# Weights' low parts on VectorE instead of GpSimd in the first seven heads of a delta-rule stage (Trainium2, one core)

## The reference, cut to what matters

```python
def gdn_mixer(h, w_in, w_conv, a_log, dt_bias, w_onorm, w_out):
    proj = h @ w_in                       # 512 x 1024 by 1024 x (4*1024 + 16)
    qkv, z, beta_logit, a_logit = jnp.split(proj, [3 * GDN_WIDTH, 4 * GDN_WIDTH, 4 * GDN_WIDTH + H], axis=-1)
    qkv = jax.nn.silu(causal_conv(qkv, w_conv))
    ...                                   # q and k are normalized per head
    o = chunk_gated_delta(q, k, v, g, beta)
    o = o * lax.rsqrt(jnp.mean(o * o, axis=-1, keepdims=True) + EPS) * w_onorm.astype(jnp.float32)
    return (o * jax.nn.silu(z)) @ w_out
```

## Time and profile before

| | |
|---|---|
| median of 3 runs | 2708.37 us (2707.45 to 2708.78) |
| the profiled execution | 2708.44 us, its span 2706.6 us |
| TensorE busy | 2662.2 us, 98% of the span |
| VectorE busy | 1387.7 us, 51% |
| ScalarE busy | 1226.5 us, 45% |
| GpSimd busy | 1075.8 us, 40% |
| granted TensorE clock | 0.999 of full speed |
| the longest chain | 70% TensorE, 6% VectorE, 2% ScalarE |

### The profile page before, as it was taken

The page is one execution under the profiler, slowest core; times in us unless marked ns, Lnnn a source line. Parts: engine busy times, 40 slices in busy tenths (PEclk is TensorE's granted clock), DMA queues, the critical chain, the costliest instruction groups (busy, mean ns, idle before and its releaser), DMA issues.

```text
span 2706.6 us, 42000 instructions
## 1 busy us (share of the span) xinstructions
PE 2662.2 (98%) x13886; PEld 2132.4 (79%) x13886; DVE 1387.7 (51%) x2452; ACT 1226.5 (45%) x1908; POOL 1075.8 (40%) x803
## 2 busy tenths in 40 slices
PE   8999999999999999999999999999999999999999
PEld 6887777777777777788887888887788877888886
DVE  7435333687778667787655221128753444222126
ACT  5334434455554555465544333235564553333234
POOL 5554333334333342443434544444412213544442
PEclk9999999999999999999999999999999999999999
DMA  4332222212021221222222333332211112333331
GB/s 159 102 101 82 82 70 77 71 55 63 31 62 51 65 74 60 86 78 70 72 68 86 101 101 93 93 112 86 78 39 49 61 31 70 109 94 93 99 102 55
DMA packets 59643, 211.89 MB, mean 78 GB/s; under 512 B 6688, under 2 KB 7072, under 8 KB 59552
## 3 DMA queue, kind: packets, MB, share of 16 engines
q1 hardware_dynamic: 57744, 206.89, 25.4%
q10 hardware_dynamic: 1520, 2.75, 0.3%
q0 software_dynamic: 288, 1.05, 0.1%
HBM read 208.57 MB, written 2.10 MB: 78 GB/s over the span
## 4 chain that ended last, share of the span: by engine, by line
PE 70%; DVE 6%; ACT 2%; issue 1%; DVEq 0%; ACTq 0%
PE bank L1329 18%; PE bank L1331 17%; PE bank L1330 17%; PE bank L3349 2%; PE bank L1458 2%; PE bank L3343 1%; PE bank L424 1%; PE bank L426 1%; PE bank L425 1%; DVE activations_low L454 1%; PE bank L1483 1%; PE bank L2199 1%; PE bank L3334 1%; PE bank L3337 1%; PE bank L3335 1%
## 5 line engine op out<-in xcount | busy, mean ns | idle before, releaser
L374 POOL TENSOR_TENSOR weights_low<-weights_raw,weights_high 128x512 fp32r<-128x512 f32 x776 | 1043.5, 1368 | 1439.7 <-ACT weights_high L358 1415.6
L1329 PE MATMUL bank<-activations_high,weights_high 128*128 128x512 f32 x2912 | 1176.3, 404 | 26.5 <-POOL weights_low L374 14.4
L1331 PE MATMUL bank<-activations_high,weights_low 128*128 128x512 f32 x2912 | 1138.6, 391 | 0.0
L1330 PE MATMUL bank<-activations_low,weights_high 128*128 128x512 f32 x2912 | 1137.4, 391 | 0.0
L1329 PEld LDWEIGHTS bank<-activations_high,weights_high 128*128 128x128 f32 x2912 | 548.4, 188 | 159.6 <-issue 18.9
L1331 PEld LDWEIGHTS bank<-activations_high,weights_low 128*128 128x128 f32 x2912 | 547.6, 188 | 116.3
L1330 PEld LDWEIGHTS bank<-activations_low,weights_high 128*128 128x128 f32 x2912 | 548.9, 189 | 108.1 <-issue 6.5
L358 ACT ACTIVATE weights_high<-weights_raw 128x1024 fp32r<-128x1024 f32 x384 | 403.8, 1053 | 283.6 <-PE bank L1331 276.7
L2980 DVE TENSOR_TENSOR mixed<-bank,mixed 128x512 f32 (+1 forms) x48 | 33.2, 692 | 193.9 <-PE bank L1331 193.9
L2924 ACT ACTIVATE to_split<-work 128x512 f32<-128x512 f32 x64 | 40.5, 632 | 181.5 <-DVE work L2966 181.5
L2966 DVE SCALAR_TENSOR_TENSOR work<-bank,rstd 128x512 f32<-128x512 f32 x64 | 44.2, 690 | 140.2 <-PE bank L1331 134.1
(11 more groups left out here) (471 smaller groups left out, 3300.3 us busy)
## 6 DMA issues: line engine op xcount, KB each, us to landing
weights_raw<-weights SPq DMA_DIRECT2D x388, 512.0 KB, 3.6
out_t<-residual SPq DMA_DIRECT2D x8, 256.0 KB, 2.1
residual<-x_t ACTq DMA_DIRECT2D x2, 512.0 KB, 7.8
residual<-x_t POOLq DMA_DIRECT2D x2, 512.0 KB, 10.0
work<-p_t ACTq DMA_DIRECT2D x2, 512.0 KB, 4.5
const<-consts SPq DMA_DIRECT2D x1, 713.0 KB, 12.8
const<-consts SPq DMA_DIRECT2D x1, 321.0 KB, 11.9
root<-positions ACTq DMA_DIRECT2D x1, 256.0 KB, 3.1
```

The source lines that it names most:

```text
L374: K.nc.gpsimd.tensor_tensor(K.w_lo[:, s, part], K.raw[:, s, part], K.w_hi[:, s, part].bitcast(F32), ALU.subtract).then_inc(K.job_sems["low ...
L1329: K.nc.tensor.matmul(dst, wh, K.act_hi[:, t, :], start=k == 0, stop=False)
L1330: K.nc.tensor.matmul(dst, wh, K.act_lo[:, t, :], start=False, stop=False)
L1331: ins = K.nc.tensor.matmul(dst, wl, K.act_hi[:, t, :], start=False, stop=k == len(tiles) - 1)
```

## The change

In the first seven heads (`more` is true) GpSimd no longer makes the low parts of the jobs r = 0 to 3. VectorE makes them, in the function `low_half(r, n, i)`: the same subtraction on the same half, with a wait on the high part and on the count of low halves so far. Two halves of r = 0 stand in levels 2 and 3, both of r = 1 behind the read of `ds6`, both of r = 2 behind the third state, both of r = 3 behind the normalization of the next query and key. GpSimd keeps the output's two products and its low part, and makes two low parts in head 7 as before. Nothing else changes; TensorE's and ScalarE's programs are the same.

```diff
--- before.py
+++ after.py
@@ -1773,9 +1773,11 @@
         weight_low(e, c0 + AHEAD + r)
 
     def head(i, more):
-        for r in range(4 if more else 2):
-            weight_low(e, c0 + 3 + AHEAD + r, i)
         if not more:
+            c = c0 + 3 + AHEAD
+            e.eng.wait_ge(K.job_sems["low"], i * (2 * SLOTS) + 2 * (c + SLOTS))
+            for r in range(2):
+                weight_low(e, c + r, i)
             return
         e.eng.wait_ge(K.sem("gdn_o_rstd"), i + 1)
         tt(b.o, b.o, b.r, ALU.mult).then_inc(K.sem("gdn_scaled"), 1)
@@ -1919,6 +1921,15 @@
     e.eng.sem_inc(K.sem("gdn_begin"), 1)
     e.eng.sem_inc(K.sem("gdn_head"), 1)
     normalize()
+
+    def low_half(r, n, i):
+
+        c = c0 + 3 + AHEAD + r
+        s, part = c % SLOTS, (slice(0, D // 2), slice(D // 2, D))[n]
+        e.eng.wait_ge(K.job_sems["high"], i * SLOTS + c + 1)
+        e.eng.wait_ge(K.job_sems["low"], i * (2 * SLOTS) + 2 * (c + SLOTS) + n)
+        v.tensor_tensor(K.w_lo[:, s, part], K.raw[:, s, part], K.w_hi[:, s, part].bitcast(F32), ALU.subtract) \
+            .then_inc(K.job_sems["low"], 1)
 
     def square_low(part, i):
 
@@ -1981,6 +1992,8 @@
             if l == 2:
                 ring.wait("qk", i)
                 ring.read("qk", v.tensor_tensor(b.qkt, by_block(ring.bank("qk")[:, :]), b.dt, ALU.mult))
+            if more and l in (2, 3):
+                low_half(0, l - 2, i)
             if l == 3 or more and l == 2:
                 take(conv, 1)
         ring.wait("vt", i)
@@ -2001,6 +2014,9 @@
         ring.wait("ds6", i)
         ring.read("ds6", v.tensor_scalar(b.sf[TOP, :, BOTTOM], by_chunk(ring.bank("ds6")[TOP, 0:NG * CH]), -1.0, None, ALU.mult))
         take(conv, 1)
+        if more:
+            low_half(1, 0, i)
+            low_half(1, 1, i)
         for c in range(NG):
             if c:
                 e.eng.wait_ge(K.sem("gdn_v_ready"), i * 3 + c)
@@ -2034,9 +2050,14 @@
                 if c == NG - 2:
                     e.eng.wait_ge(K.sem("gdn_state"), i * 3 + NG - 1)
                     e.eng.sem_inc(ring.free[ring.find("kst")[1]], 1)
+                    if more:
+                        low_half(2, 0, i)
+                        low_half(2, 1, i)
         if more:
             select(i + 1)
             normalize(i)
+            low_half(3, 0, i)
+            low_half(3, 1, i)
 
     head(0, True, True)
     with e.eng.Fori(0, H8 - 2) as k:
```

## The result

| | before | after |
|---|---|---|
| median, us | 2707.86 (22 runs, 2707.30 to 2708.86) | 2711.38 (22 runs, 2710.16 to 2714.03) |
| ratio to before, 95% interval | | 1.0014 [1.0009, 1.002] |
| profiled execution, us | 2708.44 | 2712.23 |
| its span, us; mean granted clock of TensorE | 2706.6; 0.999 | 2710.4; 0.998 |

A forecast was written before the change was run, and what follows sets the result against it. TensorE was taken to bound the loop, its parts covering the small chain almost without a gap. Terms 0 + 1.72 + 1.76 + 1.31 = 4.8 us on 2708.44 gave 2713.2 us, +0.18%, range 2711.0 to 2717.0.

The forecast's parts named there:

- GpSimd's relief is worth nothing: 72 us of halves leave GpSimd, idle for two thirds of the loop; nobody waited for them, so this counts nothing.
- A half takes 0.68, a pair 1.39: On VectorE, a half costs 0.68 us as L1926; a pair is 0.68 + 0.03 + 0.68 = 1.39 us.
- Heads 1 to 6 cost 0: In the loop VectorE's waits cover the halves, with 0.46, 0.27 and 0.73 us to spare at r = 1, 2, 3.
- the overrun rival: Loop halves run slower or register instructions between them take time: 2714.8, 2720 or 2729 us by size; chance 0.18.
- Nothing is early either: In heads 1 to 6 TensorE releases VectorE at each place, so the loop gains nothing: 0 per head.
- Head 0, 1.72 + 1.76 + 1.31: TensorE late by 1.72 us at part 17, 1.76 at part 25, and 1.31 for pair r = 3 before the next gram.
- the wide range: Whole-program time of 2711.0 to 2717.0 us, leaving out rivals faster and hidden and the far part of the overrun.
- its own case: The forecast of 2713.2 us itself, range 2712.2 to 2714.4, each of three terms within 0.3 us; chance 0.70.

The follow-up runs named there:

- before_hold: Kernel before, with GpSimd's low part of c0+5 held back ahead of head 0 until VectorE's first normalization is done: 2707.06 us, 0.9996.
- before_shift16: Kernel before, with 16 waits on a long-reached semaphore put into VectorE's head 0 where it is idle: 2707.41 us, ratio 1.0.
- again_r2: Kernel after, with one more unused 128x512 VectorE subtraction between the halves of r = 2 in heads 1 to 6: 2712.76 us, 1.0017.
- before_shift8: Kernel before, with 8 waits on a long-reached semaphore put into VectorE's head 0 where it is idle: 2706.49 us, 0.9997.
- only_head0: Kernel after, with only head 0's low halves on VectorE and those of heads 1 to 6 back on GpSimd: 2712.97 us, 1.0019.
- r1_earlier: Kernel after, with head 0's first half of r = 1 moved to level 3 from behind ds6: 2710.55 us, 1.0007.

## Why the prediction was right, and where it was off

- **GpSimd's relief is worth nothing:** right for the profiled execution of before, on which the forecast was built. VectorE's stretched lines did shrink (L1847 0.47 instead of 1.27), but each ran into a wait for TensorE. The Trainium skill, "GPSIMD Engine Reference", section "Specifications", says that the two engines share their memory interfaces. The traces agree with the stretching: L1966 takes 1.37 us beside GpSimd's low parts and 0.43 without. The relief isn't worth nothing in every execution: the stretch reached TensorE ahead of head 0, which the change doesn't touch, and once in the loop, 0.8 us, in two executions of kernels that leave these low parts to GpSimd (before_hold, before_shift16).
- **A half takes 0.68, a pair 1.39:** 0.65 to 0.70 for each of the 56; the pair 1.42 in the loop, 1.48 and 1.49 in head 0. The wait inside a pair costs a little more than taken. By the Trainium skill, "VectorE: DVE Perf Modes", section "The DRAIN you can't avoid", it would cost nothing. The traces disagree: from one half's start to the next's it is 0.60 us in again_r2, where what the second waits for is long there, and 0.73 inside a pair of the loop.
- **Heads 1 to 6 cost 0:** right, but tighter than worked out. The margins came out as 0.23 at r = 1 (0.46 forecast), 0 at r = 2 (0.27), 0.71 at r = 3 (0.73). The sum left out the gaps of 0.21 and 0.32 us ahead of a pair, though the overrun rival names such gaps. That rival's price, 0.6 us for each 0.1, was too high: of an overrun of 0.43 us at r = 2 TensorE paid 0.22 (again_r2). Its step for halves 0.4 us slower also leaves out that r = 3 would be 0.07 us late, 0.4 us more.
- **"Nothing is early either" in the loop:** by what the change moves, right; but 0.9 us came with the place of the loop's code (before_shift8).
- **Head 0, 1.72 + 1.76 + 1.31:** 1.6, 1.7 and 1.4, each at the part, the engine and the wait that was named. Sum 4.7 for 4.8.
- **What was missing in the sum** are effects of about 1 us that partly cancel: the clock's fall behind a stop, 1.6 us in the profiled execution of after, but not in every execution; the loop's code, -0.9; and the rest of the program behind the stage, -0.6 in after and -0.1 to -0.6 in the profiles of the other kernels with halves on VectorE, which no run took apart. 4.7 - 0.9 - 0.1 to 0.6 leaves 3.2 to 3.7 us without a fall of the clock; measured are 3.5, and 3.4 for the runs with a mean clock of 0.999. The missed collision ahead of head 0 belongs to the profiled execution.
- **The range:** 2711.38 lies in the wide range, but below the 2712.2 to 2714.4 that the prediction gave its own case. The three terms were each within 0.1 us; what moved the total out of the narrow range are the two last effects, for which the sum has no term.

## What to carry to other kernels

Work moved to an engine that waits is free only at places where the count of what is queued says that it comes before its user; count it for the first and the last pass through the loop as well, since the loop's margins don't hold for a head that runs ahead of the others. Moving the same eight halves of head 0 a step earlier took the 3.5 us of loss away. And a gain of less than 1 us after an edit that lengthens a program proves nothing about the edit until the same length of idle instructions has been tried.

## What of the hardware was not expected

- TensorE's granted clock fell from 2.4 to 1.2 GHz behind stops of only 1.6 to 2.0 us, in some executions and not in others with the same stops, and cost 1.6 us each time (after, only_head0 twice, r1_earlier).
- The second of two 128x512 normalizations on VectorE took 1.77 us instead of 0.69 when GpSimd's subtraction had begun 0.17 us ahead of it, and wasn't stretched when GpSimd began 0.26 us or more behind its start. GpSimd's own pair took 3.07 instead of 2.69 us in before.
- The gap between two VectorE instructions of a loop was 0.47 us in the first head and 0.23 in the other five, and 0.12 in all six with 8 waits inserted ahead of the loop.
